# Half-width products in the recurrence's block solve, sample outputs through the state as weights, and a reordered output projection

## The reference

```
layer 0:  x = x + rmsnorm( ((fox attention | memory attention) * silu(gate)) @ w_o[0] )
layer 1:  h = rmsnorm(x);  r, k, v, w, a, q_mem, gate = splits of h @ w_in
          per head (24 heads of 64), over the tokens t:
             sa = S @ (-kk_t)
             S  = S * w_t + sa (kk_t a_t)^T + v_t k_t^T
             y_t = S @ r_t
          o_tok = groupnorm(y) + bonus;  o_mem = softmax(q_mem K^T) V
          x = x + rmsnorm( ((o_tok | o_mem) * silu(gate)) @ w_o[1] )
```

## Time and profile before

| | us |
|---|---|
| median of 3 runs (1695.12 to 1702.02) | 1696.17 |
| profiled execution, its own time | 1701.55 |
| its span, first to last instruction | 1699.9 |
| PE busy | 1625.4 (96%) |
| DVE busy | 1046.9 (62%) |
| ACT busy | 404.6 (24%) |
| mean granted TensorE clock | 0.989 |

### The profile page before, as it was taken

One profiled execution on the slowest core, in us unless ns is written; L12 is line 12 of the kernel. 1 busy time (PEld: TensorE's weight loads), 2 busy tenths in 40 slices (PEclk: granted clock), 3 DMA queues, 4 the chain that ended last, 5 costly groups with the idle time before them and its releaser, 6 DMA issues.

```text
span 1699.9 us, 27940 instructions
## 1 busy us (share of the span) xinstructions
PE 1625.4 (96%) x9632; PEld 1288.7 (76%) x9632; DVE 1046.9 (62%) x4980; ACT 404.6 (24%) x1011; POOL 160.9 (9%) x295
## 2 busy tenths in 40 slices
PE   7899999899999999998999989999999999999998
PEld 6567776677677777666997867777777777788897
DVE  4787455665555655427864467777777777431755
ACT  2122111201121212121112433333333334221012
POOL 1111111121121122220000000000000000020000
PEclk9999999999999999999999999999999999999999
DMA  9689999999999999997235233333333323375341
GB/s 383 239 314 393 412 410 403 358 401 419 415 403 419 414 416 415 384 382 312 100 118 223 95 111 103 103 103 103 103 103 105 101 85 118 112 265 186 135 163 52
DMA packets 102157, 419.95 MB, mean 247 GB/s; under 512 B 41844, under 2 KB 46464, under 8 KB 92416
## 3 DMA queue, kind: packets, MB, share of 16 engines
q0 software_dynamic: 41680, 218.91, 32.4%
q1 hardware_dynamic: 54264, 189.70, 29.4%
q10 hardware_dynamic: 6072, 9.56, 1.5%
HBM read 405.28 MB, written 12.85 MB: 246 GB/s over the span
## 4 chain that ended last, share of the span: by engine, by line
PE 77%; DVE 9%; ACT 6%; DMA 6%; issue 2%; POOLq 0%; POOL 0%; ACTq 0%; DVEq 0%; SPq 0%
PE psum L757 25%; PE psum L1191 11%; PE psum L829 10%; PE psum L811 6%; PE psum L1051 5%; DMA kvr<-in_cv 3%; PE psum L746 3%; PE psum L796 2%; PE psum L1238 2%; DMA kvr<-in_ck 1%; PE psum L1248 1%; PE psum L768 1%; PE psum L780 1%; PE psum L852 1%; ACT gT L1810 1%
## 5 line engine op out<-in xcount | busy, mean ns | idle before, releaser
L1974 DVE CUSTOM_DVE_ANT_0 kvr<-kvr,arena 128x128 f32<-128x128 f32 x1488 | 323.4, 285 | 110.1 <-DMA kvr<-in_ck 110.0
L757 PE MATMUL psum<-hT,wring 128*128 128x264 f32 x1536 | 363.2, 393 | 0.0
L757 PEld LDWEIGHTS psum<-hT,wring 128*128 128x128 f32 x1536 | 290.6, 193 | 67.5 <-issue 19.8
L1191 PE MATMUL psum<-hT,kvr 128*128 128x264 f32 x1152 | 282.8, 390 | 0.0
L1191 PEld LDWEIGHTS psum<-hT,kvr 128*128 128x128 f32 x1152 | 213.4, 191 | 40.2 <-issue 6.6
L811 PE MATMUL psum<-hT,kvr 128*128 128x264 f32 x512 | 121.5, 388 | 0.0
L1974 DVE DVE_READ_ACCUMULATOR2_ANT arena<- 128x1 f32 x1488 | 120.3, 81 | 0.0
L811 PEld LDWEIGHTS psum<-hT,kvr 128*128 128x128 f32 x512 | 94.7, 190 | 15.9 <-issue 0.9
L691 POOL DMA_DIRECT2D kvr<-in_cv x128 | 67.8, 529 | 380.7 <-PE psum L1051 306.1
L1051 PE MATMUL psum<-kvr,arena 128*32 128x384 f32 x1024 | 97.6, 497 | 4.8 <-DMA kvr<-in_cv 4.8
L691 POOL DMA_DIRECT2D kvr<-in_ck x128 | 67.6, 528 | 217.2 <-issue 216.5
(11 more groups left out here) (449 smaller groups left out, 2331.9 us busy)
## 6 DMA issues: line engine op xcount, KB each, us to landing
kvr<-in_ck POOLq DMA_DIRECT2D x128, 768.0 KB, 11.5
kvr<-in_cv POOLq DMA_DIRECT2D x128, 768.0 KB, 11.1
kvr<-in_wrkv SPq DMA_DIRECT2D x12, 3072.0 KB, 11.0
kvr<-in_wo SPq DMA_DIRECT2D x14, 2048.0 KB, 8.2
wring<-in_wkv SPq DMA_DIRECT2D x12, 2048.0 KB, 11.8
wring<-in_wm SPq DMA_DIRECT2D x8, 2048.0 KB, 12.1
wring<-in_wg SPq DMA_DIRECT2D x8, 2048.0 KB, 12.1
kvr<-in_wg SPq DMA_DIRECT2D x8, 2048.0 KB, 8.8
```

The lines of the kernel that those rows point to most:

```text
L757: last = mm(psum[:, m % 2, 0:n], w[:, k, t * P:(t + 1) * P], rhs[:, k, 0:n], start=(k == 0), stop=(k == KT - 1))
L1191: last = mm(psum[:, m % 2, 0:T], w[:, k, t * P:(t + 1) * P], hT[:, k, :], start=(k == 0), stop=(k == KT - 1))
L1974: last = v_.tensor_tensor_reduce(page, page, qb[:, n % 2, h * P:(h + 1) * P], 1.0, 0.0, ALU.mult, ALU.add, S[:, n % 2, j * FH + h:j * FH + ...
```

## The change

**The block solve.** Level 0 and 1 now form only the half of the columns that is not zero. `level_w` multiplies by the lower half blocks of T (64 moving columns in place of 128, output 64 wide); ACT copies 256 columns into a new tile `WS`, zeroed once, in every second block; `level_d` forms the T side and the U side into separate banks `Vp` and `Xp` with 64 moving columns (32 for the small ones of level 1); DVE subtracts in place with two instructions of 128x256 at level 0 and of 64x128 and 128x256 at level 1. `TU16` is no longer a tile of its own. The wait on `st_out` moves from `level_d(0)` to `outputs(0)`.

**The samples' outputs.** `s3 * r`, the 512-column product, and L2477 with L2478 go. `sample_outputs` multiplies the updated state as weights (four products, 128x128 weights, 4 moving columns) by `rh`, a small tile of r per head (128x16), and four small copies bring the result into `ys`.

**The output projection.** The seven products run Q1, Q5, Q2, Q6, Q4, Q7, Q3 in place of Q1, Q2, Q4, Q6, Q5, Q7, Q3, each with the wait for its own sum; `gated(0)` to `gated(2)` move from behind `weight_sums(FEW0)` into `memory_samples()`.

**Names.** The semaphores of the weight loads are shared under `proj_in0` to `proj_in3`, with counts to match.

```diff
@@ few_products
                 if i == FEW0:
-                    pe.wait_ge(sem("u_out"), 3)
+                    pe.wait_ge(sem("u_out"), 4)
                 product(Q1, a11, b11)
+                pe.wait_ge(sem("t_sum"), 4 * layer + 1)
+                pe.wait_ge(sem("w_sum"), 4 * i + 1)
+                product(Q5, s1, t1)
                 if i == FEW0:
                     pe.wait_ge(sem("u_out"), 5)
                 product(Q2, a12, b21)
-                pe.wait_ge(sem("t_sum"), 4 * (layer + 1))
-                product(Q4, a22, t4)
+                pe.wait_ge(sem("t_sum"), 4 * layer + 2)
                 pe.wait_ge(sem("w_sum"), 4 * i + 3)
                 product(Q6, s2, t2).then_inc(sem("few_y"), 1)
-                product(Q5, s1, t1)
+                pe.wait_ge(sem("t_sum"), 4 * layer + 3)
+                product(Q4, a22, t4)
+                pe.wait_ge(sem("t_sum"), 4 * layer + 4)
                 product(Q7, s3, t3).then_inc(sem("few_y"), 1)
@@ sample_sums(1) -> sample_outputs
+                    pe.wait_ge(sem("ss_out"), o + 2)
+                    for n in range(NS // 2):
+                        last = mm(B[:, 4 * n:4 * n + 4], s0[:, a, 2 * 64 * n:2 * 64 * (n + 1)],
+                                  rh[:, 2 * n:2 * n + 2, :].rearrange("p s h -> p (s h)"), start=True, stop=True)
+                    last.then_inc(sem("ys_y"), 1)
@@ level_w, level_d
-                            last = mm(Wp[:, q * P:(q + 1) * P], NM[:, n, q, :], (TU16, TU)[n][:, q, 0:P], start=True, stop=True)
+                            last = mm(Wp[:, q * 64:(q + 1) * 64], NM[:, n, q, :], halves(TU[:, q, 0:P], n)[:, :, 0, :],
+                                      start=True, stop=True)
...
+                    for q in range(4):
+                        if n == 0:
+                            mm(Vp[:, q * 64:(q + 1) * 64], TU[:, q, P:2 * P], halves(WS[:, 0, q, :], 0)[:, :, 0, :],
                                start=True, stop=True)
+                        elif n == 1:
+                            mm(Vp[0:64, q * 32:(q + 1) * 32], TU[0:64, q, P:P + 64], WS[0:64, 1, q, 0:32], start=True, stop=True)
                     for q in range(4):
+                        if n < 2:
+                            last = mm(Xp[:, q * 64:(q + 1) * 64], WS[:, n, q, :], halves(TU[:, q, P:2 * P], n)[:, :, 1, :],
+                                      start=True, stop=True)
@@ ACT level(n)
-                            ac(Wsb, Wp, ACT.Copy).then_inc(sem("ws_out"), 1)
+                            ac(halves4(WS[:, n, :, :], n)[:, :, :, 0, :],
+                               Wp[:, 0:256].rearrange("p (q g m) -> p q g m", q=4, m=BLK * 2 ** n), ACT.Copy).then_inc(sem("ws_out"), 1)
@@ DVE level(n)
-                        tt(TU, TU16, x, ALU.subtract).then_inc(sem("tu_out"), 1)
+                        low = halves4(low, 0)[:, :, :, 0, :]
+                        tt(low, low, Vp[:, 0:256].rearrange("p (q g m) -> p q g m", q=4, m=BLK), ALU.subtract)
...
+                    tt(up, up, Xp[:, 0:256].rearrange("p (q g m) -> p q g m", q=4, m=BLK * 2 ** n), ALU.subtract)\
+                        .then_inc(sem("tu_out"), 1)
@@ DVE, the samples
+                    tt(rh, r[:, NPR:T].unsqueeze(2).to_broadcast([P, NS, 2]),
+                       blockones[:, 0:P:64].unsqueeze(1).to_broadcast([P, NS, 2]), ALU.mult)
                     tt(s3, s3, zt, ALU.add).then_inc(sem("ss_out"), 1)
-                    dve.wait_ge(sem("ss_out"), o + 2)
-                    tt(zt, s3, bs(r), ALU.mult).then_inc(sem("z_in"), 1)
                     blocks()
-                    dve.wait_ge(sem("z_y"), 2 * (o + 1) + 2)
-                    ch.do(tt(x3(Z[:, 1, :]), x3(B), i64, ALU.mult))
-                    v_.tensor_reduce(ys[:, a, :], x3(Z[:, 1, :]), AX.X, ALU.add).then_inc(sem("prepared"), 1)
+                    dve.wait_ge(sem("ys_y"), o + 2)
...
+                            last = v_.tensor_copy(ys[64 * h:64 * h + 64, a, t:NS:2], own_head[64 * t:64 * t + 64, :, 2 * t + h])
@@ DVE, memory_samples and after it
                 ts(dg1[0:32, :], ident[0:32, 0:32], m121[0:32, 0:1], None, ALU.mult).then_inc(sem("sm_dg"), 1)
+                gated(0)
...
+                gated(1)
                 dve.wait_ge(sem("sm_den"), n + 1)
                 ch.do(v_.reciprocal(rden1.rearrange("p m h -> p (m h)"), A[:, 256:288]))
+                gated(2)
...
             weight_sums(FEW0)
-            gated(0)
-            gated(1)
-            gated(2)
@@ before the first turn
+                    v_.memset(WS, 0.0)
                     v_.memset(NM, 0.0).then_inc(sem("nm_zero"), 1)
```

More of the change, by code:

```diff
@@ L415, in trunk_step @@
         ys = r1.take(2, NS)
-        Wsb = r1.take(4 * P)
+        rh = r1.take(NS, 2)
+        Wq = r1.take(4, 64)
         shout = r1.take(SHT, 1 + NS)
@@ L433, in trunk_step @@
         TUc = bk.take(4, 2, BLK)
-        TU = rg1.take(4, 2 * P)
+        WS = rg1.take(2, 4, P)
         Z = rg1.take(2, NS * 64)
@@ L512, in trunk_step, with halves, halves4 @@
         memv0 = oT[:, :, 0:NMEM]
+        def halves(x, n):
+            return x.rearrange("p (g h m) -> p g h m", h=2, m=BLK * 2 ** n)
+        def halves4(x, n):
+            return x.rearrange("p q (g h m) -> p q g h m", h=2, m=BLK * 2 ** n)
         def val(i, per, k):
@@ L555, in _, with unit @@
                 part = slice(4 * c * U, (4 * c + 4) * U)
-                sp.dma_start(wring[:, 0, part], I["wq"][0][:, part]).then_inc(sem(f"w_quarter{c}"), 16)
+                sp.dma_start(wring[:, 0, part], I["wq"][0][:, part]).then_inc(sem(f"proj_in{c}"), 16)
             sp.dma_start(cst[:, :], I["consts"]).then_inc(sem("const_in"), 16)
-            def unit(arr, index, slot, full="w_full"):
+            def unit(arr, index, slot, full=None):
                 dst = wring[:, slot, :]
@@ L564, in unit @@
                     src = arr[bass.ds(index, 1)].rearrange("a p n -> (a p) n")
-                sp.dma_start(dst[:, 0:src.shape[1]], src).then_inc(sem(f"{full}{slot}"), 16)
+                sp.dma_start(dst[:, 0:src.shape[1]], src).then_inc(sem(full or f"proj_in{2 + slot}"), 16)
             for u, (name, index, kind, first) in enumerate(UNITS):
@@ L1240, in products, with sample_sums @@
                                 last.then_inc(sem("gm_y"), 1)
-                def sample_sums(n):
+                def sample_sums():
                     if not prepare:
@@ L1246, in sample_sums, with sample_outputs @@
                     pe.wait_ge(sem("gm_out"), 4 * (o + 2))
-                    pe.wait_ge(sem("z_in"), 2 * (o + 1) + n + 1)
-                    mm((A, B)[n], blockones, Z[:, 0, :], start=True, stop=True).then_inc(sem("z_y"), 1)
+                    pe.wait_ge(sem("z_in"), o + 2)
+                    mm(A, blockones, Z[:, 0, :], start=True, stop=True).then_inc(sem("z_y"), 1)
+                def sample_outputs():
+                    if not prepare:
+                        return
+                    pe.wait_ge(sem("gm_out"), 4 * (o + 2))
+                    pe.wait_ge(sem("ss_out"), o + 2)
[3 more added lines that the diff above has]
+                    last.then_inc(sem("ys_y"), 1)
                 def level_w(n):
@@ L1266, in level_d @@
                         return
-                    if n == 0 and o:
-                        pe.wait_ge(sem("st_out"), o)
                     pe.wait_ge(sem("ws_out"), 3 * o + n + 1)
-                    if n == 1:
-                        for q in range(4):
-                            mm(X[0:64, q // 2, q % 2 * 256:q % 2 * 256 + 64], TU[0:64, q, P:P + 64], Wsb[0:64, q * P:q * P + 64],
+                    for q in range(4):
+                        if n == 0:
+                            mm(Vp[:, q * 64:(q + 1) * 64], TU[:, q, P:2 * P], halves(WS[:, 0, q, :], 0)[:, :, 0, :],
                                start=True, stop=True)
+                        elif n == 1:
+                            mm(Vp[0:64, q * 32:(q + 1) * 32], TU[0:64, q, P:P + 64], WS[0:64, 1, q, 0:32], start=True, stop=True)
                     for q in range(4):
-                        x, at0, W = X[:, q // 2, :], (q % 2) * 256, Wsb[:, q * P:(q + 1) * P]
-                        if n == 0:
-                            U = TU16[:, q, P:2 * P]
-                            mm(x[:, at0:at0 + P], U, W, start=True, stop=True)
-                            last = mm(x[:, at0 + P:at0 + 2 * P], W, U, start=True, stop=True)
-                        elif n == 1:
-                            last = mm(x[:, at0 + P:at0 + 2 * P], W, TU[:, q, P:2 * P], start=True, stop=True)
+                        if n < 2:
+                            last = mm(Xp[:, q * 64:(q + 1) * 64], WS[:, n, q, :], halves(TU[:, q, P:2 * P], n)[:, :, 1, :],
+                                      start=True, stop=True)
                         else:
-                            last = mm(Xp[0:64, q * 64:(q + 1) * 64], Wsb[64:P, q * 64:(q + 1) * 64], TU[64:P, q, P + 64:2 * P],
```

(15 more changed lines are left out.)

32 lines of the change are left out of this document (15 added, 17 removed).

## The result

The changed kernel takes 1686.85 us (median of 7 runs, 1684.83 to 1689.33), against 1695.12 of the kernel before (7 runs, 1693.99 to 1702.02). The ratio is 0.9934, 95% interval [0.9918, 0.9951]: 11.2 us less, between 8.3 and 13.9. The forecast was 12.2 us less on the profiled execution and 1684.0 in all, with 1680 to 1688 as its own range; the change measured lies in it, near its upper end.

What follows compares the result with a forecast made beforehand. PE was taken as the bound, with 77% of the chain. Turns and pipeline ends -7.8 plus output projection -4.4 made -12.2, from the median 1696.17 to 1684.0 us; forecast 1680 to 1688, wider range 1674 to 1691.5.

Steps and rivals of the forecast that it cites:

- Stage A: Turn from its last projection to `level_w(1)`, 15.61 us, PE busy 15.01; claimed -0.7 a turn, bounds -0.3 and -0.8.
- copy -0.20: ACT's copy in the block solve, 128x512 to 128x256, from 0.58 to 0.38 us, passing to DVE in full.
- subtraction -0.45: DVE's level 0 subtraction, 1.21 us for 1024 elements, becomes two of 256 taking 0.76.
- the hidden load: At `level_w(1)`, PE arriving without a wait hides its first weight load, worth 0.1 us.
- Rival 3: Block solve's moving operand in strided runs slows PE, about +3.7 us a turn, time 1728; chance 0.03.
- rival 4: Each 4-column sample product exposes its weight load, +0.75 us times 11, time 1692; chance 0.04.
- stage B: Turn from `level_w(1)` through the last projection, 26.20 us, PE busy throughout; narrower products worth 0, sample outputs +0.03.
- rival 1: Narrow block-solve products cost PE less, -0.9 us a turn in stage B; time 1672, or 1663; chance 0.10.
- PE takes over: At `level_w(1)`, PE would become the next bound, free 0.62 us earlier and arriving without a wait.
- two limits, 0.65 and 0.62: How much earlier `level_w(1)` could start: 0.65 us by the ACT and DVE chain, 0.62 by when PE is free.
- Turn 11: Pipeline's end, no preparation and PE running on; claimed -0.2 us at most, from ACT's shorter copy.
- rival 2: In the turns, ACT's and DVE's chain does not get shorter; time 1691.7, within 0.5%; chance 0.10.

Runs made afterwards that it cites:

- e7: Kernel before with only DVE's level 0 subtraction at half the columns, ACT's copy and PE at full width; ratio 0.9961, undisturbed turns 41.35 us.
- e6: Kernel before with ACT's copy and DVE's subtraction at half the columns, PE's products at full width; ratio 0.9951, undisturbed turns 41.13 us.
- e4: Kernel before with the block solve's edit alone, half columns on PE, ACT and DVE; ratio 0.9944, period 41.06 us.
- e9: Changed kernel with DVE multiplying bt and kt first, the KR parts after the level 0 subtractions; 1677.98 us, ratio 0.9899 to the kernel before.
- e5: Kernel before with the sample outputs' edit alone, the state as weights; ratio 1.0014, undisturbed turns 41.85 us.
- e11: e9 with 20 tiny unused products at PE's start to shift its instruction fetches; ratio 0.9899 to the kernel before.
- e2: Kernel before with only gated(0) to gated(2) moved into the samples' memory attention, product order as before; ratio 0.9986.
- e3: Kernel before with only the new order of the seven projection products, gate multiplications left behind the weight sums; ratio 0.9991.

## Why the prediction was right, point by point

**Stage A and the pace of PE.** The size is right. Forecast: copy -0.20, subtraction -0.45, and with PE's limit and the hidden load -0.7, period 41.15. Measured: -0.21, -0.46, -0.72, period 41.09; e7 and e6 separate the shares as 0.46 and 0.22. The row that decided it was the pace of 0.11 per instruction from the earlier trace rows. With 64 columns in strided runs the sixteen instructions of `level_d(0)` take 1.83, 0.94 and 0.89, where they took 1.86 (from 1221.83 to 1223.69, has their start), and with 4 columns eight take 0.81. The rule that the prediction quotes from the Trainium skill, TensorE: Matmul & The Clock Gate, section LDWEIGHTS, 107 ns for 128 columns of weights whatever moves, agrees with all three; the errata formula of the Trainium skill, VectorE: DVE Perf Modes, section "The TRN2 errata", max(60, 6+FD) cycles, would give 4 columns under half of what it gives 128, which no run here shows. Rival 3 and rival 4 fall with this: runs of 16 columns in the moving operand cost nothing that shows. PE's own part was forecast as the hidden load alone, 0.1. Of 0.72, stage A has 0.63 and stage B 0.09; the comparison of e6 with e4 gives the narrower products 0.08, all of it in stage B. The forecast had put that stage at nothing. The forecast's test "the prediction is wrong if stage B becomes shorter than 26.2" was drawn too sharply: 26.11 is shorter, by a tenth of what rival 1 asked for.

**What became the next limit.** The forecast said PE takes over. This step is wrong, though the number came out: DVE kept the bound. The forecast worked out when PE is free from a `turn(0)` that starts 0.20 earlier, but that start is itself set by DVE (0.18 for L2386 before), and it still is: 0.24 for its successor L2414, which a faster PE reaches sooner. ACT's gain passed to DVE in full (0.22 between e7 and e6). e9 removes the wait in front of `turn(0)`: another 0.51 a turn. That the forecast's two limits, 0.65 and 0.62, lay so close together is why the period came out right with the wrong bound.

**The ends of the pipeline.** Turn -1: forecast -0.4, measured -0.5. Turn 0: -0.5, measured -0.42. Turn 11, "-0.2 at most": this term failed, +0.60. The block solve alone gives -0.13 there (e4) and the sample edit +0.04 (e5). The rest came from where an instruction fetch fell, which e11 showed by moving it in e9; in the changed kernel itself the fetch was seen (one packet of its kind in the window of the late copies, in both of its traces) but not moved. Nothing in the forecast looked at the copies behind `Nb`, since in the turn that it read they end with slack for PE. The loss of 0.6 and the miss of 0.3 in turn 9 were outside the sum; that the total still fits is partly luck, for other terms came out larger than forecast: the undisturbed turns by 0.5 in ten, the projection by 0.2, and 0.24 in the stretch ahead of its products, which e4 has too and no term of the forecast names.

**Sample outputs.** Forecast +0.03 a turn, measured +0.03 (41.81 to 41.85 in e5, 41.06 to 41.09 between e4 and the changed kernel).

**The projection.** Forecast -4.4 with bounds -3.8 and -4.5, measured -4.6. For each half 1.7 and 3.1 was expected before e2 and e3 ran, from the same rows, and 1.57 and 3.12 measured; their sum comes close to the whole because one removes the first wait and the other nearly all behind it.

**The sum.** Forecast -12.2; by landmarks -12.1; by the ratio of the runs -11.2 with 2.8 to either side. The level of single executions moves by several us with the clock in the lead-in and turn -1, so the landmarks are the better witness. Rival 1 (1672, a ratio of 0.986) and rival 2 (1691.7, 0.997) lie outside the measured interval, and the stages exclude them by themselves.

## What to carry to other kernels

Where the weight load sets the pace of small products, halving their columns is worth what it takes off the engines before and behind them, so find out which of those chains PE waits for and cost the edit there. An idle time in a view counts from a modelled end: what a wait costs is the distance from start to start, here 0.40 where the view says 0.24. When a change of several parts is tested, compare distances between landmarks in the trace; totals of parts worth 2 to 3 us said nothing here, and each was settled to 0.1 us by the landmarks. Before naming the next bound, ask of every wait that is left which engine sets its end: here it was the one that had set the last one.

## What the runs showed of the hardware that was not expected

- A float32 product with 128x128 weights and only 4 moving columns keeps the pace of one with 64 or 128: eight instructions in 0.81 us and 0.09 more for the group behind them.
- A fetch of 16 KB of PE's instructions (77 in a run, queue q8) that falls among the eight small copies of `near` delays the step behind them by 1.1 to 1.8 us where it comes 3.6 to 4.0 us behind the first copy (5.86 and 6.48 from first issue to the next step, against 4.66 and 4.70), and by 0.7 to 1.1 where it comes 1.7 to 2.3 behind it. It hit the same turns in both traces of each program, and inserting 20 tiny products at the very start moved the long turns from 7 to 10 to 0 to 2. In the changed kernel two turns were 1.0 us too long together (0.8 in its second trace), with e9 four turns 1.7.
- The length of turn -1 jumped between 69.6 and 71.2 in traces of kernels that are the same there, with a granted clock of 0.61 in a stretch of 4 us in the longer: 1.6 us, as much as any part of the change but two.
